# Two layers written out one after the other, with the second layer's first norm moved into the first layer's last matmuls, and three small moves inside a layer

## The chip, the cores and the metric

The kernel runs on one core of a Trainium2 chip. The metric is the device time in microseconds, the median of three runs; lower is better.

## The reference, cut to what matters

The model is a two-layer network over 256 tokens with 1024 features. Each layer has three parts, each of which adds to the residual `x`:

```
for l in range(2):
    x = x + 0.5 * swiglu(rmsnorm(x, ffn1_norm[l]), ffn1_w_gate[l], ffn1_w_up[l], ffn1_w_down[l])
    h = rmsnorm(x, mix_norm[l])
    ... = split(h @ w_in[l])          # q, k, v of three attentions, index and branch gates
    y_a, y_b, y_c = DSA (top 64 keys by an index score), MoBA, NSA (compressed + selected + window)
    x = x + (g0 * y_a + g1 * y_b + g2 * y_c) @ w_out[l]
    x = x + 0.5 * swiglu(rmsnorm(x, ffn2_norm[l]), ffn2_w_gate[l], ffn2_w_up[l], ffn2_w_down[l])
return rmsnorm(x, final_norm)

swiglu(x, wg, wu, wd) = (silu(x @ wg) * (x @ wu)) @ wd        # 1024 -> 2816 -> 1024
```

All arrays are float32. Every weight is read once.

## The kernel before, in words

The kernel writes one program for each engine by hand; they meet through semaphores only. SyncE issues the weight loads, ScalarE and VectorE prepare the operands, TensorE multiplies, and GpSimd computes the scale of each norm.

Weights come in slabs of 128 x 2048 floats (1 MB; a few are smaller) in three buffers used in turn. A layer has 99 slabs: 33 for each feed-forward part and 33 for the mixer between them. Each float32 matrix product is done as three products: ScalarE rounds a slab to `whi` (`convert`, L891), VectorE subtracts for the rest `wlo` (`convert`, L418), and TensorE adds hi x hi, hi x lo and lo x hi (L1100 to L1102). A slab's buffer is loaded again when VectorE has made its `wlo` (L1446). A slab costs 24 such matmuls of 128x512.

A feed-forward part (`ffn`) goes over 11 steps of 256 hidden columns. A step has two slabs of gate and up weights (`gate_up`, into PSUM banks 0 and 1, for the first step banks 6 and 7), then the transposes of the product (`turn`, bank 2), and one slab of down weights (`down`, summed in banks 4 to 7). The steps from the second to the last but one are a loop in the program of each engine (`Fori`), and the two layers are a loop around all (L758, L844, L1084, L1434, L1503).

A part starts with the transposes of `x` (`prep`): four blocks of 256 columns, TensorE at L1116, then ScalarE multiplies with the gain and rounds to `ht_hi` (L903), and VectorE makes `ht_lo` (L427). TensorE's first product waits for `ht_lo`. The residual is added by VectorE in four pieces g = 0 to 3 (L444), each after the last matmul of its bank. For the mixer, and for the second feed-forward part, the blocks 0 and 1 are already transposed between the last matmuls of the part before (`between={3: ...}` in L1201 and L1427). Block 0 there stands ahead of piece 3 of the last slab. For the first feed-forward part of a layer they are not: `prep` of blocks 0 and 1 (L1187) comes after the last slab of the layer before.

The gains of a layer are copied by GpSimd from `cols` into `cur` at the start of each layer (L820, `cur_ready`), and other constants a little later (L827, L829, `mix_ready`). ScalarE runs a tiny activation `warm` (L1076) there. SiLU needs another activation table than the exponential of the mixer.

In the mixer the six column units of `w_in` are projected (L958 reads them out), then `fill` transposes pieces of q and k into banks 4 to 7 in turn (L1221, 13 fills). ScalarE copies out the even fills (L1035) and VectorE the odd ones (L523). TensorE does fills 0 to 4, slab 13, fills 5 to 12, slab 14. Fill 4 writes the bank of fill 0 and waits until ScalarE has copied that. In ScalarE's program slabs 13 and 14 are rounded before the read-out of unit 5 and before the first fill; in VectorE's too they stand ahead of `rope(l, 5)` and of its first fill.

The attention goes over ten slots e of one slab each. The index scores are reduced to the top 64 in eight rounds on VectorE (`select_round`, L643 and L647); the list `rounds` says how many stand at the end of each slot. After the eighth round comes `sel_b` (L650), for which TensorE waits in slot 8 (L1270).

After the second layer, ScalarE and VectorE convert one more slab, that SyncE loads from layer 0 for this (L1508 to L1511) and nobody uses.

Of the kernel before, what the change touches and what calls it, by code (L numbers as in the profile page):

```python
# [106 lines left out]
def build(nc, x_in, ffn1_w_gate, ffn1_w_up, ffn1_w_down, w_in, cmp_w1_k, cmp_w2_k, cmp_w1_v, cmp_w2_v,  # L107
# [3 lines left out]
    with ctx:  # L111
# [58 lines left out]
        cur = sb("cur", [P, 3 * KD + 32 + 3 * HD])  # L170
# [21 lines left out]
        gains = cur[:, 0:3 * KD]  # L192
        pos_c = cur[:, 3 * KD:3 * KD + 32].rearrange("p (v j) -> p v j", v=2)
        w2k = cur[:, 3 * KD + 32:3 * KD + 32 + 2 * HD]
        w2v = cur[:, 3 * KD + 32 + 2 * HD:]


# [15 lines left out]
        cur_ready = sem("cur_ready")  # L213
        mix_ready = sem("mix_ready")
# [39 lines left out]


# [142 lines left out]
        def _(dve):  # L398
# [22 lines left out]
            def prep(l, n, banks, blocks=range(4)):  # L421

                for k in [2 * b + j for b in blocks for j in range(2)]:
# [3 lines left out]
                    nc.vector.scalar_tensor_tensor(ht_lo[:, k, :], src, gains[:, n * KD + k:n * KD + k + 1],  # L427
# [21 lines left out]
            def products(l, f, i):  # L449

                r = l * 2 + f
                for t in range(NT):
# [3 lines left out]
                    bank = t + (6 if isinstance(i, int) and i == 0 else 0)  # L456
# [8 lines left out]
            def ffn(l, f):  # L465
                n, s0 = 2 * f, f * (FFN_SLABS + MIX_SLABS)
                if f == 0:
                    dve.wait_ge(cur_ready, l + 1)
                if f == 0:
                    prep(l, n, (2, 3), [0, 1])  # L470
                    convert(l, s0 + 1)
# [6 lines left out]
                def one(i):  # L478
# [6 lines left out]
                    convert(l, (r, s0 + c + 3))  # L485
# [5 lines left out]
                one(NSTEP - 1)  # L491
                residual(l, n, 4, 0.5, s0 + FFN_SLABS - 1, (2, 3) if f == 0 else None)
# [33 lines left out]
            def cmp_windows(l):  # L526

                dve.wait_ge(fill_a, l * 7 + 7)
                dve.wait_ge(mix_ready, l * 2 + 2)
                own(l)  # L530
                for v in range(2):
                    for g in range(2):
                        for a in range(2):
# [3 lines left out]
                            pb = pos_c[:, v, 8 * a:8 * a + 8].unsqueeze(2).broadcast_to([P, 8, NCMP])  # L537
# [141 lines left out]
            def mixer(l):  # L679
# [14 lines left out]
                for f in range(1, NFILL, 2):  # L694
                    fill_out(l, f)
# [8 lines left out]
                rounds = [0, 1, 1, 1, 1, 1, 1, 2, 0, 0]  # L704
# [57 lines left out]
            assert count[0] == V_STEPS, count[0]  # L762
# [10 lines left out]
        def _(pool):  # L773
# [41 lines left out]
            pool.wait_ge(setup_v, 1)  # L815
            pool.wait_ge(x_loaded, 16)
            pool.sem_inc(x_new, 4)

            def layer_gains(l):
                nc.gpsimd.tensor_copy(gains.rearrange("p (n k) -> p n k", n=3),  # L820
                                      cols[:, 0:48].rearrange("p (n c) -> p n c", n=3)[:, :, ds(l * KD, KD)])\
                    .then_inc(cur_ready, 1)

            def mixer_constants(l):

                pool.wait_ge(tables_in, TABLE_DMAS * 16)
                nc.gpsimd.tensor_copy(pos_c, cols[:, 48:112].rearrange("p (v c) -> p v c", v=2)[:, :, ds(l * 16, 16)])\  # L827
                    .then_inc(mix_ready, 1)
                nc.gpsimd.tensor_copy(cur[:, 3 * KD + 32:].unsqueeze(1),  # L829
                                      w2_all[:, ds(l, 1), :, :].rearrange("p a b c -> p a (b c)"))\  # L830
                    .then_inc(mix_ready, 1)
# [12 lines left out]
            with pool.Fori(0, DEPTH) as l:  # L844
                pool.wait_ge(x_new, l * 12 + 1)
                layer_gains(l)
                norm(l * 3)
                mixer_constants(l)
# [29 lines left out]
        def _(eng):  # L878
# [19 lines left out]
            def prep(l, n, banks, blocks=range(4)):  # L898

                for k in [2 * b + j for b in blocks for j in range(2)]:  # L900
# [3 lines left out]
                                         scale=gains[:, n * KD + k:n * KD + k + 1]).then_inc(hth, 1)  # L904
# [3 lines left out]
            def silu(l, f, i, first):  # L908
# [3 lines left out]
                for t in range(NT):  # L912
                    if not first:
                        eng.wait_ge(act_done, r * (2 * NSTEP) + i * 2 + t - 1)
                    nc.scalar.activation(sg[:, t, :], ps[:, t + (6 if first else 0), 0:FSTEP], ACT.Silu,  # L915
# [637 lines left out]
```

## Time and profile before

| | us |
|---|---|
| median of 3 runs (lowest, highest) | 1218.78 (1218.48, 1219.03) |
| the profiled execution's own time | 1215.88 |
| its span, first to last instruction | 1214.1 |
| TensorE matmul busy | 1188.5 (98%) |
| VectorE busy | 730.2 (60%) |
| ScalarE busy | 575.2 (47%) |
| GpSimd busy | 48.1 (4%) |
| HBM read | 210.33 MB, 174 GB/s over the span |

Matmuls are pipelined: one takes 0.39 us from start to end, and the next begins 0.23 us after it. So busy time alone does not say that TensorE runs at its pace; the spacing of the matmuls does. "Idle before" in a row is time in which the engine did nothing, with what ended it.

### The profile page before, as it was taken

What the parts mean: (1) busy time and instruction counts of PE and PEld (TensorE: products, weight loads), DVE (VectorE), ACT (ScalarE), POOL (GpSimd) and SP (SyncE); (2) the same over time, 40 slices, a digit from 0 to 9 for tenths busy, and PEclk for the clock granted to TensorE, in tenths of its full rate; (3) what the DMA queues carried; (4) which work ended last, traced back from release to release, by engine and by line L of the source; (5) the groups of instructions that cost most, each with busy time, mean ns of one, the idle gap of its engine ahead of it and who ended that gap; (6) DMA issues with size and microseconds to landing.
All of it is one profiled execution on the core that took longest, in us unless ns stands there. A gap on an engine that the chain in (4) does not pass through costs nothing.

```text
span 1214.1 us, 17708 instructions
## 1 busy us (share of the span) xinstructions
PE 1188.5 (98%) x5879; PEld 975.4 (80%) x5879; DVE 730.2 (60%) x878; ACT 575.2 (47%) x733; POOL 48.1 (4%) x83
## 2 busy tenths in 40 slices
PE   5999999999999999999999999999999999999997
PEld 4888888888777888888878888888887778888886
DVE  3645545858876755454555545477688776554454
ACT  5444444446654463444454444453566435544433
POOL 2000000001002000000000000000010020000000
PEclk9999999999999999999999999999999999999999
DMA  7655554664324555555546555546553235655552
GB/s 235 228 180 199 174 190 156 210 218 142 121 105 143 175 187 189 190 190 174 180 135 233 180 186 194 183 163 186 191 174 105 105 138 173 220 195 173 194 187 87
DMA packets 148011, 212.15 MB, mean 175 GB/s; under 512 B 7936, under 2 KB 109424, under 8 KB 147952
## 3 DMA queue, kind: packets, MB, share of 16 engines
q1 hardware_dynamic: 146192, 209.97, 51.1%
q10 hardware_dynamic: 1760, 1.43, 0.4%
q8 instruction: 32, 0.52, 0.2%
q14 instruction: 27, 0.22, 0.1%
HBM read 210.33 MB, written 1.05 MB: 174 GB/s over the span
## 4 chain that ended last, share of the span: by engine, by line
PE 95%; issue 2%; DVE 1%; ACT 1%; DMA 1%; ACTq 0%; DVEq 0%; POOL 0%; SPq 0%; POOLq 0%
PE ps L1100 29%; PE ps L1102 28%; PE ps L1101 28%; PE ps L1282 2%; PE ps L1172 2%; PE ps L1303 1%; PE ps L1332 1%; PE ps L1116 1%; DMA raw<-in_ffn_w_up_dram 1%; PE ps L1221 1%; PE ps L1275 0%; ACT whi L891 0%; DVE gates L664 0%; PE ps L1344 0%; PE ps L1225 0%
## 5 line engine op out<-in xcount | busy, mean ns | idle before, releaser
L418 DVE TENSOR_TENSOR wlo<-raw,whi 128x2048 fp32r<-128x2048 f32 (+2 forms) x199 | 445.7, 2245 | 227.5 <-ACT whi L891 214.7
L1100 PE MATMUL ps<-whi,ht_hi 128*128 128x512 f32 (+1 forms) x1216 | 478.6, 394 | 4.8 <-DVE ht_lo L427 4.8
L1102 PE MATMUL ps<-whi,ht_lo 128*128 128x512 f32 (+1 forms) x1216 | 471.0, 387 | 0.0
L1101 PE MATMUL ps<-wlo,ht_hi 128*128 128x512 f32 (+1 forms) x1216 | 470.2, 387 | 0.0
L891 ACT ACTIVATE whi<-raw 128x2048 fp32r<-128x2048 f32 (+2 forms) x199 | 373.0, 1880 | 169.9 <-PE ps L1102 163.5
L1100 PEld LDWEIGHTS ps<-whi,ht_hi 128*128 128x128 f32 x1216 | 228.9, 188 | 49.8 <-DVE ht_lo L427 5.5
L1102 PEld LDWEIGHTS ps<-whi,ht_lo 128*128 128x128 f32 x1216 | 228.6, 188 | 47.6
L1101 PEld LDWEIGHTS ps<-wlo,ht_hi 128*128 128x128 f32 x1216 | 229.1, 188 | 44.0
L1100 PE MATMUL ps<-whi,at_hi 128*128 128x512 f32 x336 | 131.4, 391 | 0.0
L1102 PE MATMUL ps<-whi,at_lo 128*128 128x512 f32 x336 | 130.9, 390 | 0.0
L1101 PE MATMUL ps<-wlo,at_hi 128*128 128x512 f32 x336 | 130.8, 389 | 0.0
L915 ACT ACTIVATE scr<-ps,rstd 128x256 f32<-128x256 f32 x88 | 37.0, 472 | 145.3 <-PE ps L1102 145.3
L457 DVE SCALAR_TENSOR_TENSOR scr<-ps,rstd,scr 128x256 f32<-128x256 f32 x88 | 38.5, 479 | 75.3 <-ACT scr L915 75.3
L920 ACT ACTIVATE at_hi<-ps 128x512 fp32r<-128x512 f32 x40 | 24.0, 599 | 123.9 <-PE ps L1172 123.9
L1100 PEld LDWEIGHTS ps<-whi,at_hi 128*128 128x128 f32 x336 | 63.1, 188 | 13.7 <-issue 0.8
L1102 PEld LDWEIGHTS ps<-whi,at_lo 128*128 128x128 f32 x336 | 63.1, 188 | 13.2
L1101 PEld LDWEIGHTS ps<-wlo,at_hi 128*128 128x128 f32 x336 | 63.1, 188 | 12.9
L463 DVE TENSOR_TENSOR at_lo<-ps,at_hi 128x512 fp32r<-128x512 f32 x40 | 27.7, 692 | 56.1 <-ACT at_hi L920 56.1
L990 ACT ACTIVATE prob<-ps,nmax 128x128 f32<-128x128 f32 (+1 forms) x96 | 39.3, 444 | 6.3 <-DVE nmax L580 6.3
L903 ACT ACTIVATE ht_hi<-ps,cur 128x256 fp32r<-128x256 f32 x48 | 19.3, 474 | 34.6 <-PE ps L1116 34.6
L580 DVE TENSOR_REDUCE nmax<-ps 128x4 f32<-128x512 f32 (+1 forms) x24 | 21.9, 953 | 15.6 <-PE ps L1282 15.1
L855 POOL TENSOR_SCALAR gates<-gates 128x512 f32<-128x512 f32 x24 | 18.1, 770 | 312.2 <-ACT gates L965 312.2
(161 smaller groups left out, 671.2 us busy)
## 6 DMA issues: line engine op xcount, KB each, us to landing
raw<-in_ffn_w_gate_dram SPq DMA_DIRECT2D x89, 512.0 KB, 3.7
raw<-in_ffn_w_up_dram SPq DMA_DIRECT2D x89, 512.0 KB, 4.7
raw<-in_ffn_w_down_dram SPq DMA_DIRECT2D x88, 512.0 KB, 3.8
raw<-in_w_in_dram SPq DMA_DIRECT2D x88, 512.0 KB, 4.3
raw<-in_w_out_dram SPq DMA_DIRECT2D x16, 512.0 KB, 4.0
raw<-in_w_branch_c_dram SPq DMA_DIRECT2D x8, 512.0 KB, 3.9
raw<-in_w_branch_b_dram SPq DMA_DIRECT2D x4, 512.0 KB, 4.0
raw<-in_w_branch_a_dram SPq DMA_DIRECT2D x4, 512.0 KB, 4.0
```

Of the source, the lines that this page charges most:

```text
L418: nc.vector.tensor_tensor(wlo[:, n, 0:w], raw[:, n, 0:w], whi[:, n, 0:w].bitcast(F32), ALU.subtract).then_inc(lo_done, 1)
L457: nc.vector.scalar_tensor_tensor(act[:, t, :], ps[:, bank, FSTEP:2 * FSTEP], rstd[:, t:t + 1], sg[:, t, :], ALU.mult, ALU.mult).then_inc(a ...
L463: nc.vector.tensor_tensor(lo, ps[:, 2, :], hi.bitcast(F32), ALU.subtract).then_inc(atl, 1)
L891: nc.scalar.activation(whi[:, n, 0:w], raw[:, n, 0:w], ACT.Copy).then_inc(hi_done, 1)
L915: nc.scalar.activation(sg[:, t, :], ps[:, t + (6 if first else 0), 0:FSTEP], ACT.Silu, scale=rstd[:, t:t + 1]).then_inc(silu_done, 1)
L920: nc.scalar.activation(act_parts(i)[0], ps[:, 2, :], ACT.Copy).then_inc(ath, 1)
L990: ins = nc.scalar.activation(prob_view(b, t)[:, h, :], score_head(t, h), ACT.Exp, bias=nmax[:, b, 4 * t + h:4 * t + h + 1], accum_out=den[ ...
L1100: nc.tensor.matmul(o, xh, wh, start=start, stop=False)
L1101: nc.tensor.matmul(o, xh, wl, start=False, stop=False)
L1102: return nc.tensor.matmul(o, xl, wh, start=False, stop=stop)
L1172: ins = nc.tensor.transpose(ps[:, 2, j * SEQ + t * P:j * SEQ + (t + 1) * P], act[:, t, j * P:(j + 1) * P], ident[:, :])
L1282: ins = nc.tensor.matmul(score_head(t, h), q_t[row, qb + h // 2, t * P:(t + 1) * P], k_t[row, kb + kstep * (h // 2), 0:nk], start=opens, s ...
```

## The change

The loop over layers becomes Python's `for`, so that both layers stand in the program and `l` is a number. The gains and constants are read directly from `cols` and `w2_all`, the GpSimd copies into `cur` and their waits fall. `ends(l, f)` is true for the very last part alone: for every other part the next norm's blocks 0 and 1 are transposed between the last matmuls. The first step of a first feed-forward part uses banks 4 and 5. The extra slab at the end is gone. `warm_up` is a SiLU, done once at the start and then in each second feed-forward part after its third slab. In the mixer slab 14 is rounded behind fills 0, 2, 4 (ScalarE) and behind fills 1, 3 and `rope(l, 5)` (VectorE). One selection round goes from slot 7 to slot 5.

```diff
+        def gain(l, n, k):
+            c = (n % 3 * DEPTH + l + n // 3) * KD + k
+            return cols[:, c:c + 1]
...
+        def ends(l, f):
+            return l == DEPTH - 1 and f == 1
+        def first_bank(f):
+            return 6 if f else 4
...
 # VectorE, ffn
-                if f == 0:
-                    dve.wait_ge(cur_ready, l + 1)
-                if f == 0:
+                if f == l == 0:
                     prep(l, n, (2, 3), [0, 1])
                     convert(l, s0 + 1)
...
-                residual(l, n, 4, 0.5, s0 + FFN_SLABS - 1, (2, 3) if f == 0 else None)
+                one(NSTEP - 1, ends(l, f))
+                residual(l, n, 4, 0.5, s0 + FFN_SLABS - 1, (2, 3) if not ends(l, f) else None)
...
 # VectorE, mixer
-                for m in range(2, 15):
+                for m in range(2, 14):
                     convert(l, S + m, last_width.get(S + m, SLAB))
                     if m % 2 and m < 12:
                         rope(l, m // 2 - 1)
+                for f in range(1, T1, 2):
+                    fill_out(l, f)
                 rope(l, 5)
+                convert(l, S + 14)
                 dve.wait_ge(cg_done, l + 1)
...
-                for f in range(1, NFILL, 2):
+                for f in range(T1, NFILL, 2):
                     fill_out(l, f)
...
-                rounds = [0, 1, 1, 1, 1, 1, 1, 2, 0, 0]
+                rounds = [0, 1, 1, 1, 1, 2, 1, 1, 0, 0]
...
-            with dve.Fori(0, DEPTH) as l:
+            for l in range(DEPTH):
...
 # ScalarE, ffn
-                if f == 0:
-                    eng.wait_ge(warmed, l + 1)
-                    warm_up()
-                    eng.wait_ge(cur_ready, l + 1)
-                if f == 0:
+                if f == l == 0:
+                    eng.wait_ge(setup_v, 1)
                     prep(l, n, (2, 3), [0, 1])
                     convert(l, s0 + 1)
                     prep(l, n, (2, 3), [2, 3])
                 else:
-                    prep(l, n, (4, 5))
+                    prep(l, n, (2, 3) if f == 0 else (4, 5))
                 convert(l, s0 + 2)
+                if f == 1:
+                    warm_up()
                 eng.wait_ge(rstd_ready, (l * 3 + n) * 3 + 3)
                 silu(l, f, 0, True)
...
 # ScalarE, mixer
-                for m in range(2, 15):
+                for m in range(2, 14):
...
                 project_out(l, 5)
-                eng.wait_ge(proj_done, l * 12 + 12)
-                nc.scalar.activation(cgt[:, :, :], pr[:, :, C_G:C_G + 24], ACT.Tanh, scale=0.5).then_inc(cg_done, 1)
                 for f in range(0, NFILL, 2):
+                    if f == T1 + 1:
+                        convert(l, S + 14)
+                        eng.wait_ge(proj_done, l * 12 + 12)
+                        nc.scalar.activation(cgt[:, :, :], pr[:, :, C_G:C_G + 24], ACT.Tanh,
+                                             scale=0.5).then_inc(cg_done, 1)
                     eng.wait_ge(fill_ps, l * NFILL + f + 1)
...
-                nc.scalar.activation(warm[:, :], mhalf[:, 0:1], ACT.Copy).then_inc(warmed, 1)
+                nc.scalar.activation(warm[:, :], mhalf[:, 0:1], ACT.Silu).then_inc(warmed, 1)
...
 # TensorE, ffn
-                if f == 0:
+                if f == l == 0:
                     prep(l, 0, banks, [0, 1])
...
-                if f == 0:
-                    down(l, f, last, s0 + FFN_SLABS - 1, between={3: lambda: prep(l, 1, (2, 3), [0])})
-                    prep(l, 1, (2, 3), [1])
+                if not ends(l, f):
+                    n = 2 * f + 1
+                    down(l, f, last, s0 + FFN_SLABS - 1, between={3: lambda: prep(l, n, (2, 3), [0])})
+                    prep(l, n, (2, 3), [1])
                 else:
                     down(l, f, last, s0 + FFN_SLABS - 1)
...
 # SyncE
-            v = slab(0, 4)(512)
-            sp.wait_ge(lo_done, DEPTH * LAYER_SLABS - 3 + 1 + 3)
-            for part, w in ((v[:, :, 0:FSTEP], ffn1_w_gate), (v[:, :, FSTEP:], ffn1_w_up)):
-                sp.dma_start(part, w[0, 0:512, 0:FSTEP].rearrange("(k p) c -> p k c", p=P)).then_inc(raw_in[0], 16)
```

## Rows read from the trace of the kernel before

**Rows 1.** The page's engine line, and TensorE's waits (what it waited for: us, times, longest).

```profile
PE 1188.5 (98%) x5879; PEld 975.4 (80%) x5879; DVE 730.2 (60%) x878; ACT 575.2 (47%) x733; POOL 48.1 (4%) x83
PE ps L1116 <- POOLq L817: 6.4, 1, 6.4
PE ps L1100 <- DVE ht_lo L427: 4.8, 2, 3.1
PE ps L1433 <- DMA rows<-in_rows_dram: 2.8, 1, 2.8
PE ps L1344 <- DVE gates L668: 1.7, 2, 0.8
PE ps L1116 <- DVE x L444: 0.9, 1, 0.9
PE ps L1270 <- DVE sel_b L650: 0.7, 2, 0.4
PE ps L1221 <- ACT q_t L1035: 0.7, 2, 0.3
```

**Rows 2.** Windows, last transposes to block 2: into the mixer, then into layer 1.

```profile
core 0: us, PE busy (x) PEld busy (x) DVE busy (x) ACT busy (x) POOL busy (x), PEclk, DMA share, GB/s
193.41:205.70 12.29, 12.29 (x62) 10.19 (x61) 9.24 (x11) 4.24 (x7) 0.00 (x0) 1.00 0.46 155
600.78:616.19 15.41, 12.73 (x62) 10.18 (x61) 9.06 (x11) 5.51 (x9) 0.21 (x1) 1.00 0.28 89
```

**Rows 3.** Timeline at the layer boundary (start, us, instruction, idle before).

```profile
603.85 1.28 ACT L1076 ACT_TABLE_LOAD   x1 [2.00 <-issue]
610.35 1.09 PE L1116 MATMUL ps<-ident,x 128*128 128x128 f32 x8 [0.95 <-DVE x L444]
611.04 1.57 ACT L903 ACTIVATE ht_hi<-ps,cur 128x256 fp32r<-128x256 f32 x4 [5.69 <-PE ps L1116]
612.63 1.66 DVE L427 SCALAR_TENSOR_TENSOR ht_lo<-ps,cur,ht_hi 128x256 fp32r<-128x256 f32 x4 [2.50 <-ACT ht_hi L903]
```

**Rows 4.** Timeline of ScalarE and VectorE at the first fills of layer 0.

```profile
260.33 3.93 ACT L891 ACTIVATE whi<-raw 128x2048 fp32r<-128x2048 f32 x2 [0.27 <-PE ps L1102]
264.17 0.76 ACT L958 ACTIVATE proj<-ps,rstd 128x220 f32<-128x220 f32 x2
265.11 0.85 ACT L1035 ACTIVATE q_t<-ps 128x512 f32<-128x512 f32 x2
...
262.28 4.49 DVE L418 TENSOR_TENSOR wlo<-raw,whi 128x2048 fp32r<-128x2048 f32 x2 [0.37 <-ACT whi L891]
272.34 0.69 DVE L523 TENSOR_SCALAR q_t<-ps 128x512 f32<-128x512 f32 x1 [2.44 <-PE ps L1221]
```

**Rows 5.** Timeline of TensorE there (L1221: fills 0 to 3, fill 4, from fill 5).

```profile
263.49 1.91 PE L1221 MATMUL ps<-ident,gates 128*128 128x128 f32 x16
265.74 0.65 PE L1221 MATMUL ps<-ident,gates 128*128 128x128 f32 x4 [0.34 <-ACT q_t L1035]
271.70 1.91 PE L1221 MATMUL ps<-ident,gates 128*128 128x128 f32 x16
```

**Rows 6.** Timeline of VectorE from slot 5 to the selection's end.

```profile
338.80 0.61 DVE L643 MAX8 top<-work 128x8 f32<-128x128 f32 x2
341.76 1.82 DVE L580 TENSOR_REDUCE nmax<-ps 128x4 f32<-128x512 f32 x2 [1.69 <-PE ps L1282]
355.85 0.61 DVE L643 MAX8 top<-work 128x8 f32<-128x128 f32 x2
357.03 0.66 DVE L643 MAX8 top<-work 128x8 f32<-128x128 f32 x2
358.37 0.82 DVE L650 TENSOR_SCALAR sel_b<-work 128x384 bf16<-128x384 f32 x1
```

**Rows 7.** Timeline of TensorE into slot 7 and into slot 8.

```profile
348.99 1.51 PE L1332 MATMUL ps<-p_t,proj 128*64 128x512 f32 x8
350.43 1.53 PE L1303 MATMUL ps<-ident,prob 128*128 128x128 f32 x12
...
357.37 1.51 PE L1332 MATMUL ps<-p_t,proj 128*64 128x512 f32 x8
359.24 0.39 PE L1270 MATMUL ps<-sel_b,ident_b 128*128 128x512 bf16 x1 [0.36 <-DVE sel_b L650]
```

**Rows 8.** Timeline at the start of the kernel.

```profile
11.90 2.29 DVE L418 TENSOR_TENSOR wlo<-raw,whi 128x2048 fp32r<-128x2048 f32 x1 [8.35 <-ACT whi L891]
13.31 1.55 ACT L903 ACTIVATE ht_hi<-ps,cur 128x256 fp32r<-128x256 f32 x4
14.16 1.66 DVE L427 SCALAR_TENSOR_TENSOR ht_lo<-ps,cur,ht_hi 128x256 fp32r<-128x256 f32 x4
14.70 0.80 PE L1100 MATMUL ps<-whi,ht_hi 128*128 128x512 f32 x1 [3.10 <-DVE ht_lo L427]
```

**Rows 9.** Chain of waits, pieces: turns of two loop steps, and matmuls at the start.

```profile
61.73 0.44 PE ps L1172 x4
78.52 0.44 PE ps L1172 x4
...
15.50 0.43 PE ps L1101
```

More of the change, by code:

```diff
@@ L426, in prep @@
                     src = ps[:, banks[(k // 2) % 2], (k % 2) * SEQ:(k % 2 + 1) * SEQ]
-                    nc.vector.scalar_tensor_tensor(ht_lo[:, k, :], src, gains[:, n * KD + k:n * KD + k + 1],
+                    nc.vector.scalar_tensor_tensor(ht_lo[:, k, :], src, gain(l, n, k),
                                                    ht_hi[:, k, :].bitcast(F32), ALU.mult,
@@ L477, in ffn, with one @@
                 act_rest(l, f, 0)
-                def one(i):
+                def one(i, end=False):
                     r, c = (0, 3 * i) if isinstance(i, int) else (i, 0)
@@ L484, in one @@
                         act_rest(l, f, i)
-                    convert(l, (r, s0 + c + 3))
+                    if not end:
+                        convert(l, (r, s0 + c + 3))
                     if not isinstance(i, int):
@@ L528, in cmp_windows @@
                 dve.wait_ge(fill_a, l * 7 + 7)
-                dve.wait_ge(mix_ready, l * 2 + 2)
                 own(l)
@@ L757, in _ @@
             convert(0, 0)
-            with dve.Fori(0, DEPTH) as l:
+            for l in range(DEPTH):
+                count[0] = 0
                 ffn(l, 0)
@@ L761, in _ @@
                 ffn(l, 1)
-            assert count[0] == V_STEPS, count[0]
+                assert count[0] == V_STEPS, count[0]
             gf = gr[:, 0:D]
@@ L842, in norm @@
                 nc.gpsimd.tensor_scalar(hrstd[:, :], rstd[:, :], 0.5, None, ALU.mult).then_inc(rstd_ready, 1)
-            with pool.Fori(0, DEPTH) as l:
-                pool.wait_ge(x_new, l * 12 + 1)
-                layer_gains(l)
+            for l in range(DEPTH):
                 norm(l * 3)
-                mixer_constants(l)
                 norm(l * 3 + 1)
@@ L938, in ffn, with one @@
                 act_round(l, f, 0)
-                def one(i):
+                def one(i, end=False):
                     r, c = (0, 3 * i) if isinstance(i, int) else (i, 0)
@@ L943, in one @@
                     silu(l, f, i, False)
-                    convert(l, (r, s0 + c + 3))
+                    if not end:
+                        convert(l, (r, s0 + c + 3))
                     act_round(l, f, i)
@@ L948, in ffn @@
                     one(i)
-                one(NSTEP - 1)
-                if f == 0:
+                one(NSTEP - 1, ends(l, f))
+                if not ends(l, f):
                     convert(l, s0 + FFN_SLABS + 1)
@@ L1083, in _ @@
                 eng.dma_start(dst, src).then_inc(tables_in, 16)
-            with eng.Fori(0, DEPTH) as l:
+            for l in range(DEPTH):
                 ffn(l, 0)
@@ L1199, in ffn @@
                 down(l, f, last - 1, s0 + 3 * last + 1, between={2: lambda: turn(l, f, last)})
-                if f == 0:
-                    down(l, f, last, s0 + FFN_SLABS - 1, between={3: lambda: prep(l, 1, (2, 3), [0])})
-                    prep(l, 1, (2, 3), [1])
+                if not ends(l, f):
+                    n = 2 * f + 1
+                    down(l, f, last, s0 + FFN_SLABS - 1, between={3: lambda: prep(l, n, (2, 3), [0])})
+                    prep(l, n, (2, 3), [1])
                 else:
@@ L1381, in compressed @@
                     wait_step(pe, l, ("hidden",))
[L1382 to L1383 removed]
+                    nc.tensor.matmul(ps[:, 7, K_OUT], w2k(l), hid[:, 0:32], start=True, stop=True).then_inc(cmp_ps, 1)
+                    nc.tensor.matmul(ps[:, 7, V_OUT], hid_v[:, :, :].rearrange("p h c -> p (h c)"), w2v(l), start=True,
                                      stop=True).then_inc(cmp_ps, 1)
@@ L1433, in _ @@
             nc.tensor.transpose(ps[:, 0, 0:112], rows[:, :], ident[0:112, 0:112]).then_inc(setup_pe, 1)
-            with pe.Fori(0, DEPTH) as l:
+            for l in range(DEPTH):
                 ffn(l, 0)
@@ L1501, in mixer @@
                     load_halves(l, S + m, w, r0, 2, 0, D)
-            with sp.Fori(0, DEPTH) as l:
+            for l in range(DEPTH):
                 ffn(l, 0, ffn1_w_gate, ffn1_w_up, ffn1_w_down)
```

40 lines of the change are left out of this document (13 added, 27 removed).

## The prediction

> **What bounds the kernel now.** I read the page's engine line first: TensorE is busy 98% of the span, VectorE 60%, ScalarE 47% [rows 1]. So only what TensorE does, or what it waits for, sets the end. Then TensorE's waits: they sum to 18.1 us of 1214.1, and only seven kinds exist [rows 1]. Three of them lie at the start (6.4, 2.8, and 3.1 of the 4.8). Then come the layer boundary (0.9, and the other 1.7 of the 4.8), the first fills of each mixer (0.7 in all), the selection (0.7 in all) and the gated outputs (1.7 in all). After TensorE's last matmul at 1206.6 the kernel needs another 7.5 us for the last norm and the store. The rest of the span is matmuls at a fixed spacing: two turns of the feed-forward loop lie 16.79 us apart [rows 9], and that is 72 matmuls at 0.227 us and 4 transposes at 0.11, so nothing is to be gained inside. The change can gain what the touched waits cost, and no more.
>
> **The layer boundary.** Layer 1's norm now takes the form that the mixer's norm has already. So its new cost can be read from a place in the same kernel. From the last transposes of the products to the transposes of block 2 TensorE has the same 62 matmuls in both windows: 12.29 us on the way into the mixer, all busy, and 15.41 us on the way into layer 1, 12.73 busy [rows 2]. The difference is 3.12 us, once. In detail: all of `x` has to be added before the first transpose can follow at 610.35, 0.95 us idle, then the two-engine chain of `ht_hi` and `ht_lo` makes TensorE wait again until `ht_lo` starts at 612.63 [rows 3]. The remaining 0.4 is the tail of pipelined matmuls, which counts as busy. What takes the place: pieces 2 and 3 of the last down slab now cover the chain. VectorE gets the conversion of the next slab into that cover, as in the mixer window, and is busy 9.24 us of the 12.29 there [rows 2]. ScalarE loses a table load of 1.28 us at 603.85 [rows 3]; it was idle for 5.69 us afterwards, so this is worth nothing. I take 3.1. The lower bound is the pure idle, 0.95 + 1.7 = 2.65 us; the upper is 3.3, if direct waits on constants in place of registers also shorten the hand-overs.
>
> Banks 4 and 5 for the first step: pieces 0 and 1 have left them before the first transposes may run, so no wait. The removed GpSimd copies were waited for by nobody late.
>
> At the boundary `ht_lo` begins at 612.63, though the first pair of `ht_hi` was done by about 611.9 (0.47 each from 611.04, with one spacing of 0.37) [rows 3]: 0.75 us for which the rows show no work. The Trainium skill ("Runtime: NRT & Kernel Launch", Instruction fetch mechanics) says that a taken branch to a place outside the instruction window must first fetch the page by DMA. By it this 0.75 is VectorE's jump back to the start of the layer loop, and writing the layers out removes it together with the wait; the sum stays 3.12, as the window of the mixer has no jump.
>
> **The first fills.** Fills 0 to 3 start at 263.49, fill 4 at 265.74 [rows 5]. Sixteen transposes at 0.11 would end at 265.25, so the wait costs 0.5 us, twice. Its cause: ScalarE rounds slabs 13 and 14 in one go from 260.33 to 264.26, and only then reads out unit 5 and copies fill 0 [rows 4]. With slab 14 moved, ScalarE is free at 262.3 and waits for unit 5's last matmul, which ends about 0.15 after 263.49. Read-out 0.76, copy of fill 0 0.6: done at 265.05, TensorE needs it at 265.25. That is 0.2 us to spare, so I count the full 0.5, with bounds 0.2 and 0.5. What is late next: slab 13's `wlo`, 262.28 + 2.25 = 264.5 [rows 4], needed at 265.7. VectorE now does fills 1 and 3 (1.5 us), the rope (1.6) and then slab 14's `wlo`, which ends near 270.8 instead of 266.8. TensorE wants it after fill 12, at about 276. Fill 5's copy on VectorE began at 272.34 after 2.44 us idle [rows 4], so it is not displaced. On SyncE's queue the load of slab 17 waits 4 us longer, and behind it stands the load of the compression weights, which waits for fill 12 in any case. The loads take 4.3 us from issue to landing (page, `w_in`), so slab 17 is there by 275.5, and it is rounded at 287. Sum: 2 x 0.5 = 1.0 us.
>
> **The selection.** In slot 8 TensorE waits for `sel_b`. Without a wait the work behind eight L1332 matmuls starts 1.44 us after them (348.99 to 350.43), here 1.87 (357.37 to 359.24) [rows 7]: 0.43 us, twice. A round is 1.2 to 1.3 us (355.85 to 357.03, 357.03 to 358.37) [rows 6]. With one round in slot 7, `sel_b` starts at 355.85 + 1.34 = 357.2 and ends at 358.0; TensorE wants it at 358.8. So the wait goes. The round moves to slot 5, where VectorE has 2.96 us from 338.80 to its next maxima at 341.76, of which 1.69 were idle for the scores [rows 6]. A second round of 1.3 fits with 0.4 to spare, so nothing behind it (the maxima, the exponentials of slot 6 on ScalarE that need them) moves. If it did move, it would not cost at once: its last product of slot 6 is ready 0.9 us before TensorE turns it. Sum: 2 x 0.43 = 0.9 us; bounds 0 and 0.9.
>
> **The start.** The table load and the second `warm` fall before `ht_hi` at 13.31. That looks like 1.4 us on the path to the first product at 14.70. But VectorE does slab 0's `wlo` from 11.90 to 14.19, and `ht_lo` starts at 14.16 right behind it [rows 8]. So `ht_hi` comes earlier and VectorE does not: gain 0, bounds 0 and 0.2 (SyncE's first loads issue without loop registers). The first seven matmuls are 0.43 apart instead of 0.23 [rows 9], although the clock column has 1.00 there; that stretch costs 7 x 0.2 = 1.4 us, and could end a little earlier or later than before: plus or minus 1.
>
> **Edits at nothing.** The SiLU table load in the second feed-forward part moves ahead of the wait for the norm. ScalarE waits for TensorE there afterwards in either case. The extra slab at the end (a load, 1.9 us of ScalarE, 2.3 of VectorE) ends before the last residual pieces, which wait for TensorE. The gated outputs keep their 1.7: their chain runs over VectorE and GpSimd at full load, untouched.
>
> **The sum** is made against the profiled execution, 1215.88 us (span 1214.1 and 1.8 around it): 3.1 + 1.0 + 0.9 = 5.0, hence 1210.9. The median of the runs shown is 2.9 us above the profiled one; I take this distance as it is, so 1218.78 - 5.0 = 1213.8 us.
>
> **Rivals.**
> - *Only the boundary pays.* The fills' margin of 0.2 and the selection's of 0.4 are thin, and the wait only changes its name (fill 4 for `proj`, slot 6 for its maxima). Against it: both margins come out of the same trace. 1218.78 - 3.1 = 1215.7.
> - *Stalls given back.* The boundary gain is halved, as VectorE's order (next slab before `ht_lo`) makes TensorE wait there, and the small ones give nothing: 1218.78 - 1.6 = 1217.2. Against it stands the mixer window with no idle at all.
> - *A better start.* If the slow first matmuls end earlier, or the first loads land earlier: 1.2 more, 1212.6.
> - *Inner loops pay for their place.* Slower. With two layers written out every feed-forward loop lies at its own place in the code. If a loop body straddles a border of what the engine holds, each jump back costs what the layer's jump may cost now: up to the 1.1 us between the last matmul of layer 0 and the first transpose at 610.35 beyond the normal spacing. Eight jumps are 8.9 us a part. One such part makes 1213.8 + 8.9 = 1222.7; it decides from 5.0 us lost, that is from five jumps in six of one part. Against it: the loops now run four times in two places of the code, and all turns have the spacing of [rows 9].
>
> The skill's section named above states the fetch only for targets outside the two pages held, and this is the case for which it would make this rival true. No row of this trace shows a straddling loop that pays.
>
> **The numbers.** Forecast 0.60, only the boundary 0.13, a better start 0.12, given back 0.09, inner loops 0.06. A measurement of this kernel can tell a change of about 0.2% (2.4 us) from none. Faster by over that means below 1216.3: the forecast, the better start and most of the boundary case, 0.83. Within it: 0.11. Slower: 0.06. The terms' bounds give 2.65 + 0.4 + 0 = 3.0 to 3.3 + 1.0 + 0.9 + 0.2 = 5.4, with one more for the start to either side, so 1212.4 to 1216.8. The range goes from 1211.9 to 1216.6.
>
> **What would show it.** Right: the window into layer 1 is 12.3 us for its 62 matmuls; TensorE's waits on `x` L444 and the second one on `ht_lo` are gone, as are those on `q_t` and `sel_b`; those at the start and on `gates` are as before; TensorE's last matmul ends near 1201.6. Wrong: a wait of fill 4 for ScalarE's copy; a TensorE wait for maxima or `prob` in slots 6 and 7; turns of a feed-forward loop over 16.8 us apart; a first product later than 14.7; or a median whose distance to the profiled execution is not 2.9.

## The result and the profile after

| | before | after |
|---|---|---|
| median (lowest, highest), 6 runs each on one chip, us | 1218.9 (1216.83, 1219.74) | 1209.89 (1209.27, 1210.26) |
| the profiled execution's own time, us | 1215.88 | 1209.27 |
| its span, us | 1214.1 | 1207.5 |
| its mean granted clock | 0.998 | 0.999 |

The ratio is 0.9927 (95%: 0.9915 to 0.9940): 9.0 us faster by the medians, 6.6 by the two profiled executions. The prediction was 1213.8 with a range from 1211.9 to 1216.6; the result lies below that range.

The engine line and TensorE's waits of the kernel after (us in total, times, longest), against [rows 1]:

```profile
PE 1188.0 (98%) x5879; PEld 976.0 (81%) x5879; DVE 727.4 (60%) x877; ACT 566.2 (47%) x728; POOL 46.5 (4%) x77
PE ps L1115 <- POOLq L830: 6.3, 1, 6.3
PE ps L1434 <- DMA rows<-in_rows_dram: 3.3, 1, 3.3
PE ps L1345 <- DVE gates L678: 1.7, 2, 0.8
PE ps L1099 <- DVE ht_lo L439: 0.7, 1, 0.7
```

The waits on `x`, on `q_t`, on `sel_b` and the second one on `ht_lo` are gone, and `gates` keeps its 1.7, all as forecast. One line is not as forecast: the wait for `ht_lo` at the start fell from 3.1 to 0.7.

The same two windows as [rows 2], for the kernel after:

```profile
core 0: us, PE busy (x) PEld busy (x) DVE busy (x) ACT busy (x) POOL busy (x), PEclk, DMA share, GB/s
191.66:204.02 12.36, 12.36 (x63) 10.22 (x61) 9.24 (x11) 4.20 (x6) 0.00 (x0) 1.00 0.50 162
598.17:610.54 12.37, 12.37 (x62) 10.22 (x61) 9.23 (x11) 4.20 (x6) 0.00 (x0) 1.00 0.56 183
```

The boundary window went from 15.41 to 12.37 us, all busy, and is now like the one into the mixer.

The timeline at the start, against [rows 8]:

```profile
0.86 0.44 SPq L1449 DMA_DIRECT2D raw<-in_ffn_w_gate_dram  x1
6.62 1.91 ACT L887 ACTIVATE whi<-raw 128x2048 fp32r<-128x2048 f32 x1 [2.81 <-DMA raw<-in_ffn_w_up_dram]
8.74 2.29 DVE L430 TENSOR_TENSOR wlo<-raw,whi 128x2048 fp32r<-128x2048 f32 x1 [4.65 <-ACT whi L887]
10.03 1.97 PE L1115 MATMUL ps<-ident,x 128*128 128x128 f32 x8 [6.25 <-POOLq L830]
12.12 1.67 DVE L439 SCALAR_TENSOR_TENSOR ht_lo<-ps,cols,ht_hi 128x256 fp32r<-128x256 f32 x4 [1.09 <-ACT ht_hi L899]
12.75 0.77 PE L1099 MATMUL ps<-whi,ht_hi 128*128 128x512 f32 x1 [0.75 <-DVE ht_lo L439]
```

And three rows of the same stretch of the kernel before that [rows 8] did not hold:

```profile
1.12 0.46 SPq L1448 DMA_DIRECT2D raw<-in_ffn_w_gate_dram  x1
9.79 1.91 ACT L891 ACTIVATE whi<-raw 128x2048 fp32r<-128x2048 f32 x1 [6.05 <-DMA raw<-in_ffn_w_up_dram]
9.64 1.97 PE L1116 MATMUL ps<-ident,x 128*128 128x128 f32 x8 [6.40 <-POOLq L817]
```

SyncE issues its first load 0.26 us earlier, and slab 0 is there 3.2 us earlier (9.79 to 6.62). VectorE's `wlo` is then over (11.03) before `ht_hi` exists, so the path to the first product now runs through `x`, which lands 0.4 us later than it did (its transposes at 10.03 against 9.64). The first product starts at 12.75 instead of 14.70. Counting the first 1024 packets of 1 KB on SyncE's queue (slab 0 is as many) in the two traces shows how: before, 678 had started by 5 us, and then `x`'s 4-KB packets (from 4.94) came in between until about 9; after, 1023 had started by 6 us, and `x` followed from 5.64. The last part of slab 0 landed at 9.76 before and at 6.60 after.

Setting the two profiled executions side by side matmul for matmul (5879 in each), the kernel after gains 1.75 at the start, 0.48 at each mixer's first fills, 0.41 and 0.42 at `sel_b`, and 3.02 at the layer boundary: 6.56 of the 6.6. Everywhere else the distance stands still, the inner loops included.

### The profile page after: what moved, and what is told of

The parts are those of the page before. It is cut to its first block, busy times and chain, and to the rows that moved or that the text cites. A ratio compares the mean times of both kernels' runs of the same rounds, so it can differ in the third digit from the quotient of the medians.

```text
span 1207.5 us, 16367 instructions
## 1 busy us (share of the span) xinstructions
PE 1188.0 (98%) x5879; PEld 976.0 (81%) x5879; DVE 727.4 (60%) x877; ACT 566.2 (47%) x728; POOL 46.5 (4%) x77
## 4 chain that ended last, share of the span: by engine, by line
PE 97%; DVE 1%; DMA 1%; issue 1%; ACT 0%; ACTq 0%; POOL 0%; POOLq 0%; DVEq 0%
PE ps L1099 29%; PE ps L1101 29%; PE ps L1100 29%; PE ps L1283 2%; PE ps L1172 2%; PE ps L1304 2%; PE ps L1333 1%; PE ps L1115 1%; PE ps L1222 1%; DMA x<-in_x_dram 1%; DVE gates L674 0%; PE ps L1276 0%; PE ps L1345 0%; PE ps L1226 0%; PE ps L1239 0%
## 5 line engine op out<-in xcount | busy, mean ns | idle before, releaser
L899 ACT ACTIVATE ht_hi<-ps,cols 128x256 fp32r<-128x256 f32 x48 | 19.4, 473 | 35.7 <-PE ps L1115 35.7
L590 DVE TENSOR_REDUCE nmax<-ps 128x4 f32<-128x512 f32 (+1 forms) x24 | 21.9, 953 | 15.5 <-PE ps L1283 15.3
L954 ACT ACTIVATE proj<-ps,rstd 128x512 f32<-128x512 f32 (+1 forms) x24 | 14.2, 645 | 35.7 <-PE ps L1101 35.7
```

## The experiments

Each was measured beside the kernel before on the same chip. "Before" and "after" in a heading say which kernel was edited.

**The kernel before, unchanged (e1): where do 2.4 us more come from by the medians than by the profiles?**

> The kernel before, unchanged, for its spread and a second profile. In the change 9.0 us went by the medians, 6.6 by the two profiled spans. Theory A (the start varies in the kernel before: slab 0 shares the DMA engines with x and lands anywhere from 9.8 us on): the profile's first product starts later than 14.7 whenever the time is above 1216, and the layer boundary is as before (15.4 us for its 62 matmuls). Theory B (the jump of the layer loop varies): the first product starts near 14.7 and the window at the boundary is longer than 15.4, by what the time is above 1216. Median 1218.9 plus or minus 0.5.

Measured: median 1216.77 (1216.27 to 1219.75, 12 runs). The 79 runs of this kernel that stand beside or in the experiments fall in two groups by their mean granted clock: 31 at 0.998 with a median of 1216.43 (1215.88 to 1216.91), and 48 at 0.996 (two of them at 0.997) with 1218.96 (1217.94 to 1219.91), and nothing between. The profiled execution on which the prediction rests is of the first group; the three timed runs beside it are, by their times, of the second. The kernel after has only runs at 0.998 and 0.999. The profile of e1 (1216.32) is of the first group too, so it decides between neither theory; e9 below fits neither in full.

**The kernel before, two more profiles (e9, e10): where does an execution of the second group lose its time?**

> The kernel before, unchanged, one look, to catch a run of its upper group (mean clock 0.996). Theory C, by e6: if the time is about 1218.9, the granted clock falls to half for a stretch that begins at the layer boundary, near 612 us, and the start and all else are as in the profile of the lower group. Theory D: the clock stays, and the first product starts 2.5 us late.

> As the run before it, for a second chance at the upper group. Theory C: 1216.4 with the clock kept at the boundary, or 1218.9 with a stretch at half clock there, and nothing between.

Measured: 1218.9 and 1218.05, both at 0.996. The window of 62 matmuls across the boundary in e9, and a narrower one inside it:

```profile
core 0: us, PE busy (x) PEld busy (x) DVE busy (x) ACT busy (x) POOL busy (x), PEclk, DMA share, GB/s
602.24:619.22 16.98, 14.30 (x62) 11.36 (x61) 9.61 (x11) 5.50 (x9) 0.20 (x1) 0.90 0.25 83
613.00:618.00 5.00, 3.38 (x8) 2.70 (x9) 3.74 (x5) 2.88 (x4) 0.00 (x0) 0.66 0.01 2
```

And TensorE's timeline there:

```profile
614.62 0.80 PE L1100 MATMUL ps<-whi,ht_hi 128*128 128x512 f32 x1 [1.71 <-DVE ht_lo L427]
615.22 0.63 PE L1101 MATMUL ps<-wlo,ht_hi 128*128 128x512 f32 x1
615.65 0.63 PE L1102 MATMUL ps<-whi,ht_lo 128*128 128x512 f32 x1
618.13 0.39 PE L1102 MATMUL ps<-whi,ht_lo 128*128 128x512 f32 x1
```

Idle in the window is 16.98 - 14.30 = 2.68 us, the same as in [rows 2] (15.41 - 12.73), but here the record of the clock has its lower level (1.2 GHz) from 614.62 for 3.41 us, and matmuls stand 0.43 apart instead of 0.23. The window is 1.57 us longer. The rest of the distance to the profile of before is at the start, which the expectation had as unchanged: the full clock comes at 20.7 us instead of 17.56, and TensorE is 1.4 us behind from there on. In e10 the record has the same fall, from 613.49, and the two shares are 1.3 us at the boundary and 0.9 at the start. So a little more than half of what the prediction carried over as a fixed distance was the price of an idle stretch that the change removes, and the rest that of a later rise of the clock at the start.

The two go together in the traces. In all four profiles with a fall (e6, e9, e10, e11) it comes 593.92 us after the rise at the start, wherever that was. Of the six profiles in which the layer boundary has 2.65 to 2.82 us of idle, those with the rise at 17.07, 17.56 and 18.28 (e2, before, e1) kept the clock, and those at 19.57, 20.7 and 21.0 (e10, e9, e11) lost it. Which group an execution falls in seems therefore to be settled at its start; why the rise moves is not shown.

**The kernel before, SyncE's layer loop alone written out (e2): is the start SyncE's?**

```diff
-            with sp.Fori(0, DEPTH) as l:
+            for l in range(DEPTH):
```

> The kernel before, with the layer loop written out on SyncE alone. Theory A (SyncE's first loads are issued 0.3 us earlier without the loop's registers, and slab 0 lands before x takes its share): slab 0 lands near 6.6 us, the first product starts near 12.8, and the time falls by 2 in the profile and 3 to 4 by the median, to about 1215.5. Theory B (the table load before ht_hi, or the jump): nothing at the start, 1218.9.

Measured: 1214.37 (1214.11 to 1216.67, 7 runs), ratio 0.9978 (0.9966 to 0.9990). Five of the runs are at 0.998, 1214.1 to 1214.7: 2.1 below the first group of before (the other two, at 0.996, took 1216.53 and 1216.67). The start:

```profile
6.87 1.91 ACT L891 ACTIVATE whi<-raw 128x2048 fp32r<-128x2048 f32 x1 [3.05 <-DMA raw<-in_ffn_w_up_dram]
8.99 1.28 ACT L1076 ACT_TABLE_LOAD   x1 [0.21 <-issue]
12.89 0.79 PE L1100 MATMUL ps<-whi,ht_hi 128*128 128x512 f32 x1 [0.66 <-DVE ht_lo L427]
```

Slab 0 is early, the first product is at 12.89, and the table load that the change removes here is still there and costs 0.14 us at the most (12.89 against 12.75 in the kernel after). One line on SyncE makes nearly the whole gain at the first product, 1.81 us of 1.95.

**The kernel after, SyncE held back at the start (e4): the same from the other side**

```diff
+            sp.wait_ge(setup_g, 3)
             for l in range(DEPTH):
```

> The changed kernel, but SyncE waits for three of GpSimd's first memsets before its first load, so that it issues at about 1.2 us as in the kernel before, instead of 0.86. Theory A: slab 0 shares with x again and lands at 9.5 us or later; the first product starts at 14.5 or later and the time goes up by 2 to 4 us, to 1212 to 1214. Theory B (the table load, or other things): slab 0's landing doesn't matter, 1209.9 plus 0.3.

Measured: 1212.53 (1211.84 to 1212.75, 5 runs), 2.6 above the kernel after. The start:

```profile
1.20 0.44 SPq L1449 DMA_DIRECT2D raw<-in_ffn_w_gate_dram  x1
9.93 1.91 ACT L887 ACTIVATE whi<-raw 128x2048 fp32r<-128x2048 f32 x1 [6.15 <-DMA raw<-in_ffn_w_up_dram]
14.88 0.77 PE L1099 MATMUL ps<-whi,ht_hi 128*128 128x512 f32 x1 [3.11 <-DVE ht_lo L439]
```

0.34 us later at the queue is 3.3 us later at ScalarE and 2.1 us later at the first product. The two profiled executions lie 3.45 us apart; the other 1.3 is the clock, which here rises at 20.97 instead of 16.10.

**The kernel before, all layer loops written out and nothing else (e3)**

```diff
-            with dve.Fori(0, DEPTH) as l:
+            for l in range(DEPTH):
+                count[0] = 0
...
-            with eng.Fori(0, DEPTH) as l:
+            for l in range(DEPTH):
...
-            with pe.Fori(0, DEPTH) as l:
+            for l in range(DEPTH):
```

(GpSimd's and SyncE's loops likewise.)

> The kernel before, with the layer loop written out on all five engines and nothing else changed (the norm of layer 1 still stands behind the last matmuls, with its GpSimd copies, and the small moves are not made). Theory A: as with SyncE alone at the start, and at the boundary the jumps go: the window of 62 matmuls falls from 15.4 to about 14.6 (0.75 us of VectorE's jump); 1214.8. Theory B (the jump carries the variation): the boundary gives 2 to 3 us by the median: 1216 if the start gives nothing.

Measured: 1215.79 (1214.82 to 1216.93, 11 runs, all at 0.998 or 0.999), ratio 0.9981 (0.9973 to 0.9990). It gains the start as e2 does, and 1.67 at the boundary (from the last transposes of products at 602.30 to the transposes of block 2 at 616.04: 13.74 us for the 15.41 of [rows 2]; the idle time there is 1.24 for 2.68, and the clock stayed full). But it pays 0.9 us at three first steps of a feed-forward part, and the wait of fill 4 grew (1.3 in all for 0.7), so it missed the 1214.8 by 1.0. ScalarE at one of those first steps:

```profile
436.34 1.28 ACT L916 ACT_TABLE_LOAD   x1 [3.23 <-PE ps L1103]
437.63 0.84 ACT L916 ACTIVATE scr<-ps,rstd 128x256 f32<-128x256 f32 x2
```

The table load now stands behind the wait for TensorE (3.23 us idle ahead of it) and in front of the SiLU that TensorE needs. In the loop form the same load was done ahead of that wait, in the profile of before:

```profile
432.36 1.28 ACT L915 ACT_TABLE_LOAD   x1
435.53 0.84 ACT L915 ACTIVATE scr<-ps,rstd 128x256 f32<-128x256 f32 x2 [1.89 <-PE ps L1102]
```

So without the edit of `warm_up` writing out would have given back most of what it gains.

**The kernel after, with the old warm-up (e8): what is `warm_up` as a SiLU worth?**

```diff
-                nc.scalar.activation(warm[:, :], mhalf[:, 0:1], ACT.Silu).then_inc(warmed, 1)
+                nc.scalar.activation(warm[:, :], mhalf[:, 0:1], ACT.Copy).then_inc(warmed, 1)
```

> The changed kernel with the warm-up as a copy, so that the SiLU table is loaded where SiLU is first used. My step said: hidden, 0 us, 1209.9. Theory E, from e3: in written-out layers the table load stands behind the wait for TensorE, and TensorE waits 0.83 us for it at each of three first steps: 1209.9 + 2.5 = 1212.4.

Measured: 1212.57 (1212.48 to 1213.5, 7 runs), 2.7 above the kernel after. ScalarE at the same first step, and TensorE's new wait:

```profile
434.39 1.28 ACT L911 ACT_TABLE_LOAD   x1 [3.15 <-PE ps L1101]
435.68 0.84 ACT L911 ACTIVATE scr<-ps,rstd 128x256 f32<-128x256 f32 x2
...
PE ps L1099 <- DVE wlo L430: 2.0, 3, 0.7
```

In the kernel after the load has left that place (429.75), and the SiLU follows TensorE at once:

```profile
429.75 1.28 ACT L1075 ACT_TABLE_LOAD   x1
432.98 0.84 ACT L911 ACTIVATE scr<-ps,rstd 128x256 f32<-128x256 f32 x2 [1.74 <-PE ps L1101]
```

Matmul for matmul against the kernel after, TensorE loses 0.9 us at each of the three places: the whole 2.7. TensorE's wait carries the name of `wlo`, which stands behind the late products on VectorE.

**The kernel after, with the join undone (e5): what is the boundary's gain made of?**

```diff
-                if not ends(l, f):
+                if f == 0:
                     n = 2 * f + 1
                     down(l, f, last, s0 + FFN_SLABS - 1, between={3: lambda: prep(l, n, (2, 3), [0])})
                     prep(l, n, (2, 3), [1])
...
-                if f == l == 0:
+                if f == 0:
```

> The changed kernel with the norm of layer 1 behind the last matmuls again, as before; the layers stay written out. The first runs showed two groups of times for the kernel before (about 1216.4 at a mean granted clock of 0.998, about 1218.9 at 0.996), for the changed kernel one. Theory C (the clock is taken away at the layer boundary after the idle time of 2.7 us, in part of the runs): without the jumps the idle time falls to about 2 us and the clock stays: 1209.9 + 2.4 = 1212.3, all runs at 0.998 or above. Theory D (the two groups come from the start, by where slab 0 lands): one group as well, since SyncE is early here. Either way this gives what the join is worth by itself: 3.1 less the jump's 0.75 by my steps.

Measured: 1211.67 (1211.28 to 1211.89, 4 runs), 1.8 above the kernel after, at 0.998 and 0.999. Its boundary window:

```profile
599.55:613.20 13.65, 12.49 (x63) 10.27 (x61) 8.34 (x11) 3.97 (x6) 0.00 (x0) 1.00 0.33 103
```

15.41 to 13.65 is the writing out, 1.76 us, with the direct reads of the constants in it (e3, which keeps the copies, has 1.67); 13.65 to 12.37 is the join, 1.28 us, where the expectation had 2.35. The other half microsecond of the 1.8 is no part of the boundary: in the profile the clock rises at 18.77 instead of 16.10.

The trace's single instruction records of the kernel before, which no view prints, have the jump back of the layer loop. On TensorE its record goes from 605.28 to 610.18, while the engine works off products until 609.40, and the first transposes at 610.35 in [rows 3] come right behind it. On VectorE the record itself is short (0.06), but the next instruction comes 2.87 us after its start, at 612.39, right ahead of the `ht_lo` at 612.63. In an inner loop the record on TensorE takes 0.21, and VectorE's next instruction comes after 0.17 to 0.34. In e5 the transposes follow the last product at 608.02, ahead of the last residual piece. The Trainium skill ("Runtime: NRT & Kernel Launch", Instruction fetch mechanics) has a far branch fetch its page by DMA. The trace agrees: in before its DMA records have six instruction packets (four of 8 KB, two of 16 KB) between 602.26 and 613.54, and the other profiles of the loop form (e1, e2, e9, e10, e11) have six likewise, while e3, e5 and the kernel after have none from 600 to 616 us.

**e5 with a longer pause at the boundary (e6): does the idle time itself cost the clock?**

```diff
+                if f == 1 and l == 0:
+                    nc.vector.memset(prob_all[:, :], 0.0)
```

(VectorE, behind the residual; the memset took 2.62 us.)

> The kernel of e5 with one more VectorE instruction at the end of layer 0, a memset of prob (3072 columns, about 3.2 us), so that the first ht_lo of layer 1 comes about 3 us later. Theory C: TensorE's idle time at the boundary is now about 5 us, and the granted clock falls to half there in most or all runs: besides the 3 us the time rises by another 2 to 3 us, to about 1217.8, at a mean clock of 0.996. Theory D: 1212.3 + 3 = 1215.3 at 0.998.

Measured: 1215.83 (1215.0 to 1216.12, 10 runs, all at 0.996 or 0.997), 4.2 above e5; the idle time came out shorter than the 5 us expected, and so did the sum. The window:

```profile
599.46:617.01 17.55, 14.06 (x62) 11.44 (x61) 11.92 (x12) 3.96 (x6) 0.00 (x0) 0.90 0.26 81
```

Idle rose by 3.49 - 1.16 = 2.3 us, busy by 1.57 for the same matmuls, as in e9. So with 1.16 us idle the clock stayed full in the profile of e5, and every run had the high mean; with 2.7 it fell in the two profiled executions of the 0.996 group (and 48 of 79 runs belong to that group); with 3.49 it fell in the profiled one, and every run had the low mean.

**The kernel after, fills and selection undone (e7), and the selection alone (e14)**

```diff
-                for m in range(2, 14):
+                for m in range(2, 15):
...
-                for f in range(1, T1, 2):
-                    fill_out(l, f)
...
-                convert(l, S + 14)
...
-                rounds = [0, 1, 1, 1, 1, 2, 1, 1, 0, 0]
+                rounds = [0, 1, 1, 1, 1, 1, 1, 2, 0, 0]
```

(e7: all of it, ScalarE's part too; e14: the last two lines alone.)

> The changed kernel with slab 14 and the selection round back in their old places. By the prediction's steps both waits come back: 2 x 0.5 + 2 x 0.43 = 1.9 us, 1211.8. A rival: written out, the first fills' wait is longer (in e3 fill 4 waited 1.07 and 0.57 us beyond its spacing instead of 0.51 twice), so 2.4 us, 1212.3.

> The changed kernel with the selection round back in slot 7 and nothing else. By my step 2 x 0.43 more: 1210.8. By e3 and e7 (no wait for sel_b with the rounds in their old places, once the layers are written out, because VectorE's sel_b begins just ahead of GpSimd's instruction and takes 0.36 us): 1209.9, no difference.

Measured: e7 1211.52 (1211.11 to 1211.73, 4 runs), 1.6 above the kernel after. Matmul for matmul the first fills lose 0.65 in each layer, and the wait for `sel_b` does not come back. TensorE at the fills of e7, then `sel_b`, GpSimd beside it, and TensorE behind it:

```profile
265.26 0.65 PE L1216 MATMUL ps<-ident,gates 128*128 128x128 f32 x4 [0.40 <-ACT q_t L1028]
...
357.88 0.36 DVE L660 TENSOR_SCALAR sel_b<-work 128x384 bf16<-128x384 f32 x1
357.88 1.42 POOL L848 TENSOR_SCALAR gates<-gates 128x512 f32<-128x512 f32 x2 [18.42 <-ACT gates L958]
358.38 0.38 PE L1265 MATMUL ps<-sel_b,ident_b 128*128 128x512 bf16 x1
```

e14: 1210.26 (1209.15 to 1212.42, 5 runs), no measurable distance from the kernel after. Its profiled execution is the one of 1212.42:

```profile
0.86 0.44 SPq L1449 DMA_DIRECT2D raw<-in_ffn_w_gate_dram  x1
10.06 1.91 ACT L887 ACTIVATE whi<-raw 128x2048 fp32r<-128x2048 f32 x1 [6.26 <-DMA raw<-in_ffn_w_up_dram]
...
359.18 0.36 DVE L660 TENSOR_SCALAR sel_b<-work 128x384 bf16<-128x384 f32 x1
```

`sel_b` takes 0.36 here too and nobody waits for it, with the round where it was before. And its start shows the other thing: SyncE issued at 0.86, as in the kernel after, and slab 0 was late all the same. All 3.1 us of this execution's distance are at the start. The landings show a single straggler: a load lands in 16 parts, slab 0 is two loads, and 31 of the 32 parts were there by 6.45 us, the last one at 10.04. In the eight other profiles with the early issue and `x` behind it slab 0 was complete between 6.60 and 7.42. The early landing is likely, not certain.

**The kernel before with the moved round alone (e11)**

```diff
-                rounds = [0, 1, 1, 1, 1, 1, 1, 2, 0, 0]
+                rounds = [0, 1, 1, 1, 1, 2, 1, 1, 0, 0]
```

> The kernel before, with the selection round moved from slot 7 to slot 5 and nothing else. My step: the waits for sel_b go, 2 x 0.43, so 0.9 us less in either group: 1215.6 and 1218.0. In e3 and e7 those waits were gone with the rounds in their old places, where sel_b took 0.36 us instead of 0.82: there VectorE began it just ahead of GpSimd's instruction on the gates and not just behind it. A rival from that: here sel_b comes earlier than GpSimd's instruction and takes 0.36 as well.

Measured: 1218.0 (1215.25 to 1218.32, 10 runs), ratio 0.9992 (0.9983 to 1.0002). In its profile both waits on `sel_b` are gone (0.41 each); its one run at 0.998, 1215.25, stands against 1216.43. In the loop form the waits go as predicted, and the medians can't tell the move from nothing. `sel_b` starts earlier there and also takes 0.36 us, as GpSimd is not at work beside it, so e11 does not tell which of the two ended the wait.

**Towards a better version: `x` first and other gates (e12), slab 1 behind `x` (e13)**

```diff
+                    if l == f == 0 and a == 1:
+                        sp.wait_ge(x_loaded, 16)
```

(e13, SyncE ahead of slab 1. e12 instead issues `x` before the 64-KB table and interleaves the two gated outputs of the last slots.)

> The changed kernel with two more edits. ScalarE issues the load of x ahead of a table of 64 KB; in the profile after, slab 0 is there at 6.6 us and x at 10.0, so x holds the start: it should land 0.6 us earlier, unless it takes that from slab 0. And VectorE gates the first two pieces of branch A ahead of the last piece of branch C (bank 7), since TensorE waits 0.9 us for them in each layer (the 994 and 1000 ns beyond the spacing at L1345): 0.6 to 0.9 less each, unless GpSimd's additions then slow VectorE. Sum 1.8 to 2.4: 1207.5 to 1208.1.

> The changed kernel, but SyncE issues slab 1 only when x has landed. If x is now what sets the first product (12.7 us, with x at 10.0), it lands up to 0.6 us earlier, because the 0.23 MB of slab 1 that share the engines with it are gone; slab 1 has until about 17 us. 1209.3, unless slab 1 (or slab 2 behind it) comes late: then a wait of TensorE at its 25th product, and 1210 or more. If the start is set by slab 0 alone, 1209.9.

Measured: e12 1212.65 (1212.24 to 1213.21, 5 runs), a miss of 2.8. `x` landed earlier, at 8.1, and shared the queues with slab 0, which was then late (9.40):

```profile
9.40 1.91 ACT L889 ACTIVATE whi<-raw 128x2048 fp32r<-128x2048 f32 x1 [5.59 <-DMA raw<-in_ffn_w_up_dram]
```

The gates' wait fell from 1.0 to 0.63 us, with a new one of 0.8 and more right behind it, so each layer lost 0.6. e13: 1208.67 (1208.45 to 1209.75, 5 runs), ratio to before 0.9924 (0.9911 to 0.9938), 1.2 below the kernel after:

```profile
12.20 0.77 PE L1099 MATMUL ps<-whi,ht_hi 128*128 128x512 f32 x1 [0.75 <-DVE ht_lo L439]
```

The first product is at 12.20 for 12.75. It is the fastest version that was run; it was not measured side by side with the kernel after, and the ranges overlap at 1209.27 to 1209.75.

## Why the prediction was wrong

By its own steps:

- **The layer boundary: right in size, wrong in make-up.** 3.12 forecast, 3.02 to 3.04 measured. The comparison with the mixer's window gave the sum without needing a cause. The cause was mostly the writing out (1.76 by e5, 1.67 by e3) and less the join (1.28). The 0.75 us for which I saw no work was too small a share for the jump: TensorE's wait, which the profile puts down to `x`, ended with TensorE's own jump too.
- **The first fills: right.** 0.5 each forecast, 0.48 measured, 0.65 in e7.
- **The selection: right in size (0.43 each; 0.41 and 0.42), wrong in cause for this kernel.** The waits go with the move alone (e11), but the change does not need it (e14). In the kernel before `sel_b` took 0.82 us [rows 6], with GpSimd's `gates` begun 15 and 17 ns ahead of it. With the layers written out (e3, e7, e14) the two begin within 5 ns, and it takes 0.36. I had taken 0.82 as its duration.
- **The edit of the SiLU table load, "edits at nothing": the time came out right, the reason did not.** I wrote that ScalarE waits for TensorE afterwards in either case. With the layers written out the load would have stood behind that wait, for 2.7 us (e8), 0.9 at each of three places. The price of leaving the edit away was not in the old trace, where the load ran ahead of the wait. The extra slab, the gates and the inner loops are as forecast.
- **The start: the step that failed in the profile.** "Gain 0, bounds 0 and 0.2 (SyncE's first loads issue without loop registers)": it was 1.75 between the profiles, 2.1 by the medians of e2 and 2.6 by those of e4. I had the right edit and passed on its 0.26 us one to one. The row that mattered, slab 0 landing at 9.79 just when `x` did (9.64), was read as a fact and not as a collision: two transfers that end together had been sharing. The rival "a better start" names "the first loads land earlier", with 1.2 us. The slow first matmuls were read off a window's clock column, which says 1.00; the record of the full clock begins at 17.56 only, so they ran at the lower level. The plus or minus 1 for them was fair: the rise came between 15.3 and 21.0 us over all profiles.
- **The distance of 2.9 from the profiled execution to the median: "I take this distance as it is".** It was the step that failed in the medians. 2.5 us of it is the distance between the groups (1218.96 - 1216.43): 1.3 to 1.6 for the clock's fall behind the idle stretch at the boundary and 0.9 to 1.4 for the later rise at the start (e10, e9). The kernel after has no such idle stretch and no run in the second group: its median is 0.6 above its profiled execution.

In sum 5.0 forecast against 6.6 in the profiles, 1.6 short, nearly all at the start (1.75 for 0); and 2.3 short in the distance: 3.9 us together, 1213.8 against 1209.9. The range failed for the second reason, as no bound of it had the distance move: 2.3 us lower its lower end would be 1209.6 and take in the result, 1.75 us lower it would be 1210.2 and would not. The terms' own bounds add up to 1212.4 to 1216.8; the range stated, 1211.9 to 1216.6, is not that sum, and neither of the two reaches down to the result.

Left open: why one part of slab 0 lands late in an execution with an early issue (e14), why the clock's rise at the start moves, and with it whether the idle of 2.7 us costs the clock, and why ScalarE's table load stands ahead of the wait in the loop form.

## What to carry to other kernels

Where the profiled execution and the median differ by more than the runs of one kind do, sort all runs by their mean granted clock before carrying the distance over: a part of it can be the price of the very stall that a change removes. Where two transfers land together at a start, take their order as a thing that a few tenths of a microsecond at the issue can turn, and bound it by the whole overlap. When a loop is written out, look for what its jump cost (here 1.67 to 1.76 us) and for what had crept ahead of a wait because of it (here a table load worth 2.7 us if it isn't placed by hand).

## What the runs showed of the hardware that was not expected

- A first load issued 0.26 us earlier was complete 3.2 us earlier, by keeping ahead of another queue's transfer; it is a race (converted from 6.62 in the kernel after, from 10.06 in e14, both issued at 0.86). In e14 one of the 32 parts of the slab landed 3.6 us behind the other 31.
- TensorE's granted clock fell to its lower level for 3.41 us behind the idle stretch at the boundary: not with 1.16 us idle (e5) or 1.24 (e3), in e9, e10 and e11 but not in the profiles of before, e1 and e2 with 2.7, and with 3.49 (e6). The price was 1.57 us in the windows of e9 and e6 and 1.3 in e10. The fall came 593.92 us after the rise in all four. The rise to full clock at the start lay between 15.3 and 21.0 us over all profiles.
- VectorE's `sel_b` of 128x384 to bf16 took 0.36 us alone (after). Where GpSimd's `gates` had begun 11 to 20 ns before it (ten times in the loop form: before, e1, e2, e9, e10) it took 0.81 to 0.82 and GpSimd's 0.62; where the two began within 5 ns (six times: e3, e7, e14) it took 0.36 and GpSimd's 0.84. The loss of one engine is 0.46, that of the other 0.22.
- The jump back of the layer loop took 4.9 to 5.5 us on TensorE in six profiles, against 0.21 in an inner loop; in before, queued products covered all of it but the last microsecond. On VectorE the next instruction came 2.8 to 3.0 us after it, against 0.17 to 0.34. Six instruction packets lay around the far jump in each of the six, and none where the layers are written out (e3, e5, after).
